# Attention with scores computed in two orientations, and the output product in two parts

## The reference

```
s = (einsum('bhqd,bkhd->bhqk', qn, k_nope) + einsum('bhqr,bkr->bhqk', qr, k_rope)) * scale
mask = k_chunk[None, :] <= q_chunk[:, None]
s = jnp.where(mask, s, -1e30)
pr = jax.nn.softmax(s, axis=-1)
o = einsum('bhqk,bkhv->bhqv', pr, v)
```

## Time and profile before

| | us |
|---|---|
| median of 3 executions | 757.61 (754.63 to 757.69) |
| the profiled execution | 756.21 |
| its span | 754.2 |
| PE busy | 659.0 (87%) |
| DVE busy | 342.3 (45%) |
| ACT busy | 260.4 (35%) |
| POOL busy | 12.1 (2%) |
| mean granted clock of PE | 0.939 |
| read from HBM | 173.17 MB, 231 GB/s over the span |

### The profile page before, as it was taken

The page is one execution under the profiler, slowest core; times in us unless marked ns, Lnnn a source line. Parts: engine busy times, 40 slices in busy tenths (PEclk is TensorE's granted clock), DMA queues, the critical chain, the costliest instruction groups (busy, mean ns, idle before and its releaser), DMA issues.

```text
span 754.2 us, 10432 instructions
## 1 busy us (share of the span) xinstructions
PE 659.0 (87%) x4102; PEld 472.8 (63%) x4104; DVE 342.3 (45%) x625; ACT 260.4 (35%) x441; POOL 12.1 (2%) x49
## 2 busy tenths in 40 slices
PE   5999996999999999979996639949999995868895
PEld 3999984999999999947874424534444441324342
DVE  5686936587766667652634640251111110102133
ACT  5762536465555555443254320101111110100143
POOL 1000002000000000000000000000000000000000
PEclk9999998899999999989998858959999999989999
DMA  9844345555666651087353054348879999999911
GB/s 328 303 156 179 114 140 216 151 168 184 208 204 202 201 170 56 0 311 260 121 213 113 2 235 209 137 198 323 347 316 429 427 428 425 427 426 428 401 55 56
DMA packets 54341, 174.71 MB, mean 232 GB/s; under 512 B 4646, under 2 KB 29346, under 8 KB 47906
## 3 DMA queue, kind: packets, MB, share of 16 engines
q1 hardware_dynamic: 53632, 172.54, 59.8%
q10 hardware_dynamic: 674, 1.69, 0.6%
HBM read 173.17 MB, written 1.05 MB: 231 GB/s over the span
## 4 chain that ended last, share of the span: by engine, by line
PE 73%; DMA 13%; DVE 9%; ACT 3%; issue 2%; DVEq 0%; ACTq 0%
DMA arena<-in_w_moe_dram 12%; PE ps L1526 12%; PE ps L1527 11%; PE ps L1528 11%; PE ps L1948 6%; PE ps L1879 4%; PE ps L1721 4%; PE ps L2029 4%; PE ps L1958 3%; PE ps L1934 3%; PE ps L1983 3%; PE ps L1711 2%; PE ps L1756 1%; DMA hh<-in_conv_ffn_dram 1%; PE ps L1796 1%
## 5 line engine op out<-in xcount | busy, mean ns | idle before, releaser
L1526 PE MATMUL ps<-hT_high,w_up_high 128*128 128x256 f32 x352 | 100.4, 285 | 2.5 <-DVE w_up_low L1106 2.5
L1527 PE MATMUL ps<-hT_low,w_up_high 128*128 128x256 f32 x352 | 100.1, 284 | 0.0
L1528 PE MATMUL ps<-hT_high,w_up_low 128*128 128x256 f32 x352 | 100.1, 284 | 0.0
L1526 PEld LDWEIGHTS ps<-hT_high,w_up_high 128*128 128x128 f32 x352 | 68.2, 194 | 3.8 <-DVE w_up_low L1106 3.4
L1527 PEld LDWEIGHTS ps<-hT_low,w_up_high 128*128 128x128 f32 x352 | 68.2, 194 | 0.3
L1528 PEld LDWEIGHTS ps<-hT_high,w_up_low 128*128 128x128 f32 x352 | 68.1, 193 | 0.0
L1106 DVE TENSOR_TENSOR w_up_low<-W,w_up_high 128x1024 fp32r<-128x1024 f32 x44 | 52.8, 1227 | 25.3 <-ACT w_up_high L716 25.3
L716 ACT CAST w_up_high<-W 128x1024 fp32r<-128x1024 f32 x44 | 44.6, 1047 | 29.9 <-PE ps L1528 29.9
L1948 PE MATMUL ps<-W,junk 128*32 128x512 f32 x352 | 41.4, 612 | 5.1 <-DMA W<-in_w_moe_dram 5.1
L1526 PE MATMUL ps<-h_high,dense_high 128*128 128x256 f32 x160 | 45.7, 286 | 0.0
L853 ACT ACTIVATE arena<-ps 128x256 f32<-128x256 f32 x9 | 3.5, 384 | 122.1 <-PE ps L1948 122.1
(11 more groups left out here) (404 smaller groups left out, 1168.7 us busy)
## 6 DMA issues: line engine op xcount, KB each, us to landing
W<-in_w_moe_dram SPq DMA_DIRECT2D x27, 2048.0 KB, 20.6
arena<-in_w_moe_dram SPq DMA_DIRECT2D x17, 2048.0 KB, 27.8
W<-in_w_up_dram SPq DMA_DIRECT2D x22, 1024.0 KB, 8.2
W<-in_w_in_dram SPq DMA_DIRECT2D x8, 2048.0 KB, 10.9
W<-in_w_down_dram SPq DMA_DIRECT2D x11, 1024.0 KB, 4.9
hh<-in_w_moe_dram SPq DMA_DIRECT2D x4, 2048.0 KB, 28.6
W<-in_w_out_dram SPq DMA_DIRECT2D x2, 2048.0 KB, 9.0
W<-in_w_o_dram SPq DMA_DIRECT2D x2, 2048.0 KB, 10.6
```

The source lines that it names most:

```text
L1526: pe.matmul(o, lhs[0], rhs[0], start=first, stop=False, skip_group_check=True)
L1527: pe.matmul(o, lhs[0], rhs[1], start=False, stop=False, skip_group_check=True)
L1528: return pe.matmul(o, lhs[1], rhs[0], start=False, stop=last_k, skip_group_check=True)
```

## The change

The change computes the attention scores twice. The first time (SA, six groups) the queries are on partitions; DVE takes from PSUM only the negated maximum over the keys that a query sees (two reductions per group, since the second half of a block sees 64 keys more). Four small products turn the maxima into two rows of eight (in duplicate, at partitions 0 and 64), and ACT and DVE write them as a rounded high part and a remainder (nm). The second time (ST, six groups) the keys are on partitions. PSUM collects three things: a product of a selector (selr) with nm, which puts the query's negated maximum in every row, a bf16 product of one row that puts the mask on the first chunk, and the scores. ACT takes one exponential per group straight from PSUM to SBUF (EA, EB), and this is the stationary operand of the value product (attend), whose moving operand is v2 with a column of ones for the row sum. DVE divides the 64 values (attended), and four transposes per token half bring the output to hT.

The gate rows move ahead of the low-rank queries on PE, and their DVE part ahead of the rotary multiplications. The w_o product is split: for each token half first the four attention parts of the contraction, with the head transposes between the halves, then the four recurrent parts. ACT loads the table of the root before it is needed. POOL builds selector, mask row and the ones of v2 ahead of its copy of the rotary part. SP's issues of items 3 to 6 wait for other semaphores. The core of the diff:

```diff
+        SA = ((0, 0, 4, 4), (0, 4, 4, 5), (1, 0, 2, 6), (1, 2, 2, 7), (1, 4, 2, 0), (1, 6, 2, 1))
+        ST = ((0, 0, 2), (0, 2, 2), (1, 0, 4), (0, 4, 2), (0, 6, 2), (1, 4, 4))
+        PV = ((0, 0, 3), (1, 0, 4), (0, 1, 5), (1, 1, 7))
...
-            for n, (name, count) in enumerate((("xm_used", 1), ("zw_used", 1), ("uq_used", 1), ("wm_used", 1),
-                                               ("pv_done", 8), ("pv_done", 8), ("pv_done", 8),
+            for n, (name, count) in enumerate((("xm_used", 1), ("zw_used", 1), ("uq_used", 1), ("st_done", 6),
+                                               ("pv_done", 4), ("at_ready", at("at_ready", 2)), ("num_done", 4),
...
+            pool.memset(mrow[0:1, 0:CH], 0.0).then_inc(sig("sel_built"), 1)
+            pool.memset(mrow[0:1, CH:P], 1.0).then_inc(sig("sel_built"), 1)
+            pool.memset(mrow[0:1, P:3 * P], NEG).then_inc(sig("sel_built"), 1)
+            pool.memset(selw, 0.0).then_inc(sig("sel_built"), 1)
+            pool.wait_ge(sig("sel_built"), 4)
+            pool.tensor_copy(nm, selw[:, 0:256]).then_inc(sig("sel_built"), 1)
+            pool.wait_ge(sig("sel_built"), 5)
+            for n in range(2):
+                pool.affine_select(out=v3(selw[0:64 * n + 8], A_HEADS), in_=v3(selw[0:64 * n + 8], A_HEADS), compare_op=ALU.not_equal,
+                                   fill=1.0, base=-64 * n, pattern=[[-1, A_HEADS], [0, P]],
+                                   channel_multiplier=1).then_inc(sig("sel_built"), 1)
+                pool.wait_ge(sig("sel_built"), 6 + n)
+            pool.tensor_copy(selr, selw).then_inc(sig("sel_built"), 1)
+            pool.wait_ge(sig("sel_built"), 8)
 
             pool.wait_ge(sig("kr_ready"), at("kr_ready", 1))
             pool.tensor_copy(kTa[64:128, 1:A_HEADS, :], kTa[64:128, 0:1, :].broadcast_to([2 * ROPE, A_HEADS - 1, SEQ]))\
...
-                act.copy(v2[:, b, :], ps[:, b, :]).then_inc(sig("v2_ready"), 1)
+                act.copy(v2[:, b, :, 0:VD], v3(ps[:, b, :], A_HEADS)).then_inc(sig("v2_ready"), 1)
...
+            act.wait_ge(sig("nt_done"), at("nt_done", 1))
+            act.wait_ge(sig("sel_built"), 5)
+            for r in (0, 64):
+                act.copy(nm[r:r + A_HEADS], ps[r:r + A_HEADS, 7, 0:256]).then_inc(sig("nm_high"), 1)
             for h in range(M_HEADS):
                 act.activation(xcT[:, h, :], xcT[:, h, :], ACT.Copy, scale=par_c("ml_skip_2", h)).then_inc(sig("skip_ready"), 1)
+
+            for n, (kb, h, heads) in enumerate(ST):
+                act.wait_ge(sig("st_done"), n + 1)
+                act.activation((EA, EB)[kb][:, h:h + heads, :], v3(ps[:, n % 2, :], heads), ACT.Exp).then_inc(sig("e_ready"), 1)
+            act.activation(small[:, 8:9], epsc[:], ACT.Sqrt).then_inc(sig("table_ready"), 1)
+            for b in range(TB):
+                act.wait_ge(sig("oT_done"), at("oT_done", b + 1))
+                act.copy(hT[:, 0:4, b * P:(b + 1) * P], v3(ps[:, b, :], 4)).then_inc(sig("at_ready"), 1)
...
-            def softmax_in(i):
...
-                m = amask[:, P:2 * P] if b == 0 else amask
-                link(dve.tensor_tensor(sP[i % 2][:, :, 0:nk], v3(ps[:, i % 2, 0:2 * nk], 2),
-                                       m.unsqueeze(1).broadcast_to([P, 2, nk]), ALU.add))
-                dve.tensor_reduce(amx[i % 2], sP[i % 2][:, :, 0:nk], AX, ALU.max, negate=True).then_inc(sig("s_ready"), 1)
...
-            def softmax_out(i):
-                nk = P * (i % 2 + 1)
-                dve.wait_ge(sig("e_ready"), 2 * i + 2)
-                link(dve.reciprocal(asum[i % 2], asum[i % 2]))
-                dve.tensor_tensor(sP[i % 2][:, :, 0:nk], sP[i % 2][:, :, 0:nk],
-                                  asum[i % 2].unsqueeze(2).broadcast_to([P, 2, nk]), ALU.mult).then_inc(sig("p_ready"), 1)
...
+                m = v3(ps[:, bank, 0:heads * nk], heads)
+                dve.wait_ge(sig("sa_done"), at("sa_done", n + 1))
+                dve.tensor_reduce(nmax[:, b, h:h + heads], m[:, :, 0:nk - CH], AX, ALU.max, negate=True).then_inc(sig("max_ready"), 1)
+                dve.tensor_reduce(nmaxh[CH:P, b, h:h + heads], m[CH:P, :, nk - CH:nk], AX, ALU.max, negate=True)\
+                   .then_inc(sig("max_ready"), 1)
+            dve.wait_ge(sig("max_ready"), at("max_ready", 2 * len(SA)))
+            dve.tensor_tensor(nmax[CH:P], nmax[CH:P], nmaxh[CH:P], ALU.min).then_inc(sig("nmax_ready"), 1)
...
+            def attended(n):
+
+                b, hq, bank = PV[n]
+                o = v3(ps[:, bank, 0:4 * (VD + 1)], 4)
+                r = rsum[:, b, 4 * hq:4 * hq + 4]
+                dve.wait_ge(sig("pv_done"), n + 1)
+                link(dve.reciprocal(r.unsqueeze(2), o[:, :, VD:VD + 1]))
+                dve.tensor_tensor(v3(otok[:, b, 256 * hq:256 * hq + 256], 4), o[:, :, 0:VD],
+                                  r.unsqueeze(2).broadcast_to([P, 4, VD]), ALU.mult).then_inc(sig("o_ready"), 1)
+
+            dve.wait_ge(sig("nm_high"), at("nm_high", 2))
+            dve.tensor_tensor(nm[64:64 + A_HEADS], ps[64:64 + A_HEADS, 7, 0:256], nm[64:64 + A_HEADS].bitcast(F32),
+                              ALU.subtract).then_inc(sig("nm_ready"), 1)
+            weigh(0)
+            weigh(1)
+            divide(0)
+            weigh(2)
+            divide(1)
+            attended(0)
+            attended(1)
+            weigh(3)
+            divide(2)
+            divide(3)
+            attended(2)
+            attended(3)
...
+            pe.wait_ge(sig("gates_ready"), at("gates_ready", 1))
...
+            for n, row in ((0, 0), (1, 2)):
...
+            for n in range(2):
...
-                free = (("csq_ready", 1), ("gi_ready", 1), ("xm_ready", 1), ("xm_ready", 2))[hp]
+                free = (("warg_ready", 4), ("gi_ready", 1), ("ucol_ready", 1), ("warg_ready", 2))[hp]
...
+            gate(0, (2, 3), "mq_done", ((("qn_ready", 3), ("qr_ready", 3)), (("qn_ready", 4), ("qr_ready", 4))))
+
+            pe.wait_ge(sig("krope_spread"), 1)
+            pe.wait_ge(sig("kn_ready"), at("kn_ready", 4))
+            for n, (b, h, heads, bank) in enumerate(SA):
+                nk = P * (b + 1)
+                if n >= 4:
+                    pe.wait_ge(sig("v2_ready"), at("v2_ready", n - 3))
+                for hh in range(heads):
+                    last = pe.matmul(ps[:, bank, nk * hh:nk * hh + nk], qTa[:, h + hh, b * P:(b + 1) * P], kTa[:, h + hh, 0:nk],
+                                     start=True, stop=True)
+                last.then_inc(sig("sa_done"), 1)
+
+            gate(1, (2, 3), "mk_done", ((("mq_ready", 1),), (("mq_ready", 2),)))
...
-                    last.then_inc(sig("pt_done"), 1)
...
-                    for hh in range(2):
-                        h = 2 * hp + hh
-                        for kb in range(b + 1):
-                            last = pe.matmul(ps[64 * hh:64 * hh + 64, 4 + hp % 2, b * P:(b + 1) * P],
-                                             v2[:, kb, h * VD:(h + 1) * VD], PTs[g % 2][:, (b + 1) * hh + kb, :],
-                                             start=(kb == 0), stop=(kb == b), skip_group_check=True)
...
+            def turned_scores(n):
+
+                kb, h, heads = ST[n]
+                nq = 512 // heads
+                o = v3(ps[:, n % 2, :], heads)
+                if n < 2:
+                    pe.wait_ge(sig("max_ready"), at("max_ready", 10 + 2 * n))
+                else:
+                    pe.wait_ge(sig("e_ready"), at("e_ready", n - 1))
+                for hh in range(heads):
+                    pe.matmul(o[:, hh, :], v3(selr, A_HEADS)[0:72, h + hh, :], nm[0:72, kb * P:SEQ], start=(hh == 0), stop=False,
+                              skip_group_check=True)
+                pe.matmul(o[:, :, 0:CH], mrow[0:1, 0:P], mrow[0:1, P:P + CH * heads], start=False, stop=False, skip_group_check=True)
+                for hh in range(heads):
+                    last = pe.matmul(o[:, hh, :], kTa[:, h + hh, kb * P:(kb + 1) * P], qTa[:, h + hh, kb * P:SEQ], start=False, stop=True,
+                                     skip_group_check=True)
+                last.then_inc(sig("st_done"), 1)
+
+            def attend(n):
+
+                b, hq, bank = PV[n]
+                pe.wait_ge(sig("e_ready"), at("e_ready", 3 * hq + 2 + b))
+                if n == 0:
+                    pe.wait_ge(sig("mv_ready"), at("mv_ready", 2))
+                o = v3(ps[:, bank, 0:4 * (VD + 1)], 4)
+                for kb in range(b + 1):
+                    for hh in range(4):
+                        h = 4 * hq + hh
+                        e = EB[:, h, :] if kb else EA[:, h, b * P:(b + 1) * P]
+                        last = pe.matmul(o[:, hh, :], e, v2[:, kb, h, :], start=(kb == 0 and hh == 0), stop=(kb == b),
+                                         skip_group_check=True)
+                last.then_inc(sig("pv_done"), 1)
...
+            pe.wait_ge(sig("nmax_ready"), at("nmax_ready", 1))
+            for b in range(TB):
```

(58 more changed lines are left out.)

259 lines of the change are left out of this document (93 added, 166 removed).

## The result

The changed kernel takes 729.48 us (727.63 to 730.47), the kernel before 757.48 beside it: a ratio of 0.9629, 95% interval 0.9603 to 0.9655, 28.0 us faster. The forecast was 738.9 with a range from 730 to 751. The direction was right, the gain came from the places that were named, and the size was missed by 9.4 us, half a microsecond past the low end. All medians and ratios are of executions at the usual granted clock; one of e11_order_only, 1119.41 us at a granted clock of 0.557, is left out.

What follows compares the result with a forecast made beforehand. PE, held in the attention's dependency ring, bounds the part before the expert stage, the weight stream its end. At full clock 24.6 gained, less 5.6 for clock and 0.3 for POOL: 18.7 off 757.61 gives 738.9, range 730 to 751.

Steps and rivals of the forecast that it cites:

- What bounds the kernel, and what reaches the end: Before the first expert product at 510 us: the weight stream restarts on what PE frees, so gains there count in full.
- rival 4: Whole kernel: the expert weight stream is the bound, so the change does not reach the end, 757; chance 0.04.
- Up to v2: Gate rows moved ahead: same work, nothing gained; the 1.8 of low clock behind them kept, v2 ends at 392.9.
- POOL: POOL's added selects beside DVE's norm at 323 to 328: cost 0.3 taken, bounds 0 to 2.3.
- Scores and the turn: First scores on PE 12.0 in one piece, maxima hidden with 2.2 to spare; turn of the maxima 1.7.
- Turned scores and value product: PE's second making of scores through the value products: 19.0, plus 1.5 waiting before num(3), ending at 427.1.
- the bound of 2.6: Turned scores: most that mask row and mixed kinds in one bank might add over 16 rounded products; 0 taken.
- The overlap of w_o: Head norm runs beside the first w_o products: some 10 of the 24.6 gained at full clock.
- The clock's share: From 392.9 through w_o: mean clock 0.86 until w_o, and half of w_o's 2.6 lost; 5.6 in all.
- rival 1: Attention stretch and w_o: the clock stays at 1.00, 24.3 gained, 733.3; chance 0.20.
- Rival 2: Attention stretch and w_o: clock stays at 0.72, or late divisions or no overlap; 10.1 gained, 747.5; chance 0.18.
- Rival 3: First scores to last value product at clock 0.50: 9.1 later, 766.7; turning point mean clock 0.58; chance 0.06.

Runs made afterwards that it cites:

- e11_order_only: Changed kernel with the third group's value product ahead of num(3) and DVE's divisions to match, POOL unchanged: 727.72 us, ratio 0.9614.
- The fillings: Kernel before, with 20 bf16 products or eight fp32 transposes put into each of PE's eight waits for DVE's division: 755.93 us and 755.56 us.
- the slow exponentials: Changed kernel with each of the six exponentials of the turned scores made eight times, so PE waits for ACT: 746.23 us.

## Why the prediction came out as it did

**What bounds the kernel, and what reaches the end.** Right. From the first expert product to the end it takes 243.99 where it took 244.06, the stream is down to 27 GB/s over 473 to 485, and full at 425 over the same 157 us, now 26.5 earlier. What was gained ahead counted in full; rival 4 is out.

**Up to v2.** The order of the gate rows was right, and the 1.8 that I carried along with them was not lost: v2 ends 15.5 behind the z panels (mq's start), not 17.2. This is the smaller part of what was mis-sized; the rows put back show that the place of the rows has a part in it, and the one exception that it isn't all.

**POOL.** I took 0.3 within 0 to 2.3; by experiment it is 0.58 at DVE and 0.26 further on. Two selects took 2.37 together, not 2.3 each: my price by elements was twice too high, since the row it came from had 4 partitions and 512 columns in 1.15 and these have 8 and 1024 in 1.19.

**Scores and the turn.** In one piece as said, 11.3 instead of 12.0, and 1.3 instead of 1.7 from the turned maxima to the first turned score. The maxima ended at 401.5, 2.2 before mv's product was through, as forecast.

**Turned scores and value product.** 19.0 and a wait of 1.5 were forecast, 21.1 in all measured with a wait of 1.39. The chain has a pair of heads (selector, mask, scores):

```profile
407.21 0.24 PE ps L1883 x2
407.44 0.16 PE ps L1885
407.60 1.06 PE ps L1887 x4
```

The rounded products cost their spacing of 0.12, as taken; the mask row 0.16 instead of 0.06, and the scores behind it 1.06 instead of 0.89. So a pair took 1.46, not 1.19, and a group of four 1.70, not 1.56: 1.4 more in all, inside the bound of 2.6, of which I had taken 0. The value products gave 1.0 back: twelve took 2.63, so 0.22 each and not 0.26. The two errors nearly cancel; the first pair's selector rows took 0.50 instead of 0.24.

**The overlap of w_o.** Right: start to y2 28.6 against 28.9, with the head norm hidden; and 9.5 from the split by the traces against 10.

**The clock's share.** This is the step that failed. The sum at full clock was 82.1 from the z panels to y2, 80.3 without the dip, and 79.9 was measured. To it I added 4.3 in the stretch, for a mean clock of 0.86, and 1.3 in w_o, and neither was lost: 1.00 was granted throughout. These 5.6 are the larger part of the 9.4 that the forecast missed. The 0.86 was the middle between two levels of the old kernel, as if the level went in proportion to PE's load. The fillings and the slow exponentials show that it doesn't: the level fell behind waits of 2 to 4 us, and with such waits gone there was nothing to interpolate. (The dip behind the gate rows is a fall without such a wait, and its cause stays open.) The longest waits in the new stretch are 1.39, 0.74 and 0.46, and the clock stayed at 1.00 across them.

So rival 1 was the case, which I gave 733.3 and a chance of 0.20. Measured was 3.8 less: the dip that wasn't there 1.8, the router 1.3, and the rest the small terms above; the first two rows of the table and the place of the profiled executions nearly cancel. The router's 1.3 is luck: the forecast had taken it as fixed, and it falls one way or the other from trace to trace. The range's low end had been made from rival 1 and 3 us, and left the dip out, since I had counted it as certain work.

**The other rivals.** Rival 2's cause, waits that keep the clock low, is real: the unsplit w_o and the slow exponentials show it. This order of work has no wait that long. Rival 3 had a turning point at 0.58, and nothing came near it.

## What to carry to other kernels

Cost a reordered stretch at full clock and ask for each wait that it leaves how long the engine stands still there (here 1.4 us left the clock alone, waits of 2 to 4 us mostly did not); a mean level taken between an idle and a busy stretch of the old kernel prices nothing. When a ring of dependencies is broken up, the clock comes back as a second gain on top of the waits (here the 5.6 us that I had written off), while filling the waits with idle work brings the clock back and leaves the ring (some 3 us). And a stall seen once behind some instruction (1.8 us behind the gate rows) belongs into the range, not into the sum.

## What was not expected of the hardware

- The half level outlasts its cause: PE busy for 9.86 of 10 us had a granted clock of 0.67 behind two waits of 2.3 and 2.2 us, and the first sixteen instructions of w_o took 9.31 us instead of 7.11 right behind the old loop.
- fp32 transposes kept the clock up like bf16 products did: 0.84, 1.00, 1.00 in the same three windows.
- The dip behind eight products of K = 4, between 1.6 and 1.8 us: in all five traces with them behind v2, in one of eight with them ahead of the low-rank queries, though PE's order up to there is the same in those eight.
- Kinds mixed in one bank took longer on PE than alone: two fp32 products of 256 columns took 1.06 behind the bf16 mask row, where two in a row take 0.89, and the mask row itself 0.16. Whether the change of kind or the shared bank costs it, no run separates.
- The same router code took 26.4 to 26.9 us in six traces and 27.7 in seven, and its granted clock had come back earlier in the six.
